# Thirty-two experts fed from HBM: a seventh unit staged ahead, and the staged loads asked for by GpSimd's queue

## What is computed

```python
def moe_ffn(h, w_router, b_router, w_gate_up, b_gate_up, w_down, b_down):
    xt = h.reshape(T, D)                                  # 256 x 1024
    logits = (xt @ w_router) + b_router                   # 32 experts
    top_v, top_i = lax.top_k(logits, TOP_K)               # 4 of them per token
    gates = jax.nn.softmax(top_v, axis=-1)
    ...
    def expert_block(args):
        xb, e = args
        hdn = xb @ w_gate_up[e] + b_gate_up[e]            # 1024 x 2048 weights
        return clamped_swiglu(hdn) @ w_down[e] + b_down[e]  # 1024 x 1024 weights
    ...
    out = jnp.zeros((T, D), y.dtype).at[tok_sorted].add(y[dest] * g_sorted[:, None])

def clamped_swiglu(hdn):
    x_glu = jnp.minimum(hdn[..., :D_EXPERT], SWIGLU_LIMIT)
    x_lin = jnp.clip(hdn[..., D_EXPERT:], -SWIGLU_LIMIT, SWIGLU_LIMIT)
    return x_glu * jax.nn.sigmoid(SWIGLU_ALPHA * x_glu) * (x_lin + 1)
```

## Time and profile before

| what | value |
|---|---|
| median of 3 runs | 2068.12 us (2065.26 to 2071.54) |
| the profiled execution | span 2064.6 us from the first to the last instruction; the page gives no other time of it |
| median less span | 3.5 us |
| PE busy | 1945.9 us, 94% |
| POOL busy | 589.1 us, 29% |
| HBM read | 607.17 MB |
| expert stage | from about 226 us to about 1204 us of the span |

### The profile page before, as it was taken

One profiled execution on the slowest core, in us unless ns is written; L12 is line 12 of the kernel. 1 busy time (PEld: TensorE's weight loads), 2 busy tenths in 40 slices (PEclk: granted clock), 3 DMA queues, 4 the chain that ended last, 5 costly groups with the idle time before them and its releaser, 6 DMA issues.

```text
span 2064.6 us, 28177 instructions
## 1 busy us (share of the span) xinstructions
PE 1945.9 (94%) x10657; PEld 1193.4 (58%) x10658; DVE 892.1 (43%) x1387; ACT 721.6 (35%) x1182; POOL 589.1 (29%) x622
## 2 busy tenths in 40 slices
PE   5998899989999999999999889999999999999998
PEld 2975333323333333333332269788888898898887
DVE  4645312111222221111211156557797575576983
ACT  2544111101111111111111055664665466646662
POOL 3230243443342433424433504000233021000440
PEclk7998899999999999999999989999999999999999
DMA  9999599999898999999999965345456554544653
GB/s 341 299 360 367 227 420 417 417 418 418 342 419 326 419 418 417 367 395 417 419 417 417 418 230 200 123 152 196 152 190 208 169 185 132 174 170 137 197 194 120
DMA packets 203044, 609.34 MB, mean 295 GB/s; under 512 B 10458, under 2 KB 115054, under 8 KB 166384
## 3 DMA queue, kind: packets, MB, share of 16 engines
q1 hardware_dynamic: 197360, 585.14, 74.2%
q0 software_dynamic: 5280, 22.19, 3.1%
q10 hardware_dynamic: 328, 0.95, 0.1%
HBM read 607.17 MB, written 9.26 MB: 299 GB/s over the span
## 4 chain that ended last, share of the span: by engine, by line
PE 69%; DMA 11%; SPq 7%; DVE 6%; ACT 4%; issue 2%; POOL 1%; ACTq 0%; DVEq 0%
PE bank L903 21%; PE bank L1256 14%; PE bank L940 10%; DMA side<-in_w_gate_up 9%; PE bank L1280 8%; PE bank L942 5%; SPq L740 5%; PE bank L1207 2%; SPq L747 2%; PE bank L1220 1%; DMA ring<-in_w_down 1%; DVE split L1739 1%; PE bank L1010 1%; PE bank L1248 1%; ACT split L2167 1%
## 5 line engine op out<-in xcount | busy, mean ns | idle before, releaser
L1256 PE MATMUL bank<-ring,qkv 128*64 128x512 f32 x2240 | 502.9, 597 | 34.0 <-POOL ring L2423 33.9
L1256 PEld LDWEIGHTS bank<-ring,qkv 128*64 128x64 f32 x2240 | 151.8, 137 | 367.0 <-issue 265.1
L1739 DVE TENSOR_TENSOR split<-ring,split 128x2048 fp32r<-128x2048 f32 x104 | 249.1, 2395 | 115.4 <-ACT split L2167 115.3
L940 PE MATMUL bank<-hT_both,split 128*128 128x512 f32 x800 | 283.2, 399 | 7.1 <-DVE split L1739 7.1
L1280 PE MATMUL bank<-ring,qkv 128*64 128x512 f32 x1120 | 248.5, 595 | 1.2 <-DMA ring<-in_w_down 1.0
L2167 ACT ACTIVATE split<-ring 128x2048 fp32r<-128x2048 f32 x104 | 199.1, 1915 | 130.9 <-PE bank L903 126.2
L942 PE MATMUL bank<-hT_both,split 128*128 128x256 f32 x800 | 223.6, 280 | 0.0
L1713 DVE TENSOR_SCALAR qkv<-bank 128x512 f32<-128x512 f32 x35 | 24.2, 692 | 443.5 <-PE bank L1256 443.5
L2139 ACT ACTIVATE qkv<-qkv 128x512 f32<-128x512 f32 x35 | 22.1, 631 | 533.5 <-DVE qkv L1713 533.5
L1727 DVE SCALAR_TENSOR_TENSOR out_halves<-bank,small,out_halves 64x512 fp32r<-64x512 f32 x70 | 52.5, 750 | 332.3 <-ACT out_halves L2150 331.8
L940 PEld LDWEIGHTS bank<-hT_both,split 128*128 128x128 f32 x800 | 151.6, 189 | 44.6 <-DVE split L1739 8.4
(11 more groups left out here) (363 smaller groups left out, 3045.5 us busy)
## 6 DMA issues: line engine op xcount, KB each, us to landing
ring<-in_w_down SPq DMA_DIRECT2D x150, 1024.0 KB, 17.2
ring<-in_w_gate_up SPq DMA_DIRECT2D x70, 1024.0 KB, 20.4
probs<-in_w_gate_up SPq DMA_DIRECT2D x62, 1024.0 KB, 18.0
ring<-in_w_in SPq DMA_DIRECT2D x58, 1024.0 KB, 5.5
ring<-in_w_up SPq DMA_DIRECT2D x44, 1024.0 KB, 5.1
qkv<-in_w_gate_up SPq DMA_DIRECT2D x31, 1024.0 KB, 21.7
consts<-in_w_gate_up SPq DMA_DIRECT2D x31, 1024.0 KB, 20.5
side<-in_w_gate_up SPq DMA_DIRECT2D x31, 1024.0 KB, 22.4
```

The source lines that it names most:

```text
L940: pe.matmul(b[:, :].rearrange("p (h t) -> p h t", h=2), w_high[:, k, rows], hT_both[:, :, k, :], start=(k == 0), stop=False, skip_group_ch ...
L1256: last = pe.matmul(hidden[q][CAP * j:CAP * j + CAP, :], xgT[:, k % 4, k // 4, :], unit_at(k)[:, c:c + 512], start=False, stop=(k == KC - 1 ...
L1739: dve.tensor_tensor(low, unit_at(u % RING_L), high.bitcast(F32), ALU.subtract).then_inc(low_done, 1)
```

## The change

`STAGED` becomes 7: unit 6 gets a second buffer too. Its memory comes from scratch rows that now share: `glu` lies on `xrow`, `act_row` and `brows` on `sig`, and `bdown` on the new staged buffer. Since `glu` and `xrow` are one row, ACT's `rows_out` waits until DVE has made the activation (`act_ready`). SP asks for expert 1's unit 6 once the slot tables are filled (`slots_filled`). The staged loads of experts 2 to 31 are no longer issued by SP: POOL issues each right behind its own copy of the same unit of the expert before (`load_staged`, behind a wait for that copy and one more one-column add), and signals them in `landed_staged`; the ones of expert 1 stay with SP and signal in `landed_early`. SP's loop only has `load_direct(e)`, for units 7 to 11. POOL's loop is cut into expert 1, experts 2 to 30 and expert 31.

```diff
-STAGED = 6
+STAGED = 7
...
-        xrow, glu, lin, sig = (moe(512) for _ in range(4))
-        bdown, staged_qkv = moe(D)[0:EXPERTS, :], moe(UNIT)
+        xrow, sig = (moe(512) for _ in range(2))
+        staged_qkv = [moe(UNIT) for _ in range(2)]
+        bdown = staged_qkv[0][0:EXPERTS, 0:D]
         assert at[0] <= 6144
-        brows, act_row = glu, lin
+        glu, brows, act_row = xrow, sig, sig
...
-        staged_at = [probs_t[:, 0:UNIT], probs_t[:, UNIT:2 * UNIT], hT_t[:, :], const("bands"), staged_qkv, side[:, :]]
+        staged_at = [probs_t[:, 0:UNIT], probs_t[:, UNIT:2 * UNIT], hT_t[:, :], const("bands"), staged_qkv[1], side[:, :], staged_qkv[0]]
...
-            def load_staged(e, u):
-                sp.dma_start(staged_at[u], hidden_rows(e)[:, u, :]).then_inc(landed_staged[u], 16)
+            def load_early(u):
+                sp.dma_start(staged_at[u], hidden_rows(1)[:, u, :]).then_inc(landed_early[u], 16)
...
             sp.wait_ge(*full("logits4"))
-            load_staged(1, 2)
+            load_early(2)
             sp.wait_ge(*emptied("list"))
+            sp.wait_ge(slots_filled, 1)
+            load_early(6)
             load_direct(1)
             with sp.Fori(2, EXPERTS) as e:
-                for u in range(STAGED):
-
-                    sp.wait_ge(landed_moe[u], e + 15)
-                    load_staged(e, u)
                 load_direct(e)
...
             def rows_out(n):
                 act.wait_ge(gathered, n)
+                if type(n) is not int or n > 1:
+                    act.wait_ge(act_ready, n - 1)
                 act.activation(xrow, banks[6][:, :], ACT.Copy).then_inc(xrow_ready, 1)
...
-            with pool.Fori(1, EXPERTS) as e:
+
+            def load_staged(e, u):
+
+                pool.wait_ge(landed_moe[u], e + 15)
+                pool.tensor_tensor(passed[:, STAGED + 1 + u:STAGED + 2 + u], zeros[:, 0:1], zeros[:, 0:1], ALU.add)
+                rows = w_gate_up[0, bass.ds(e, 1)].rearrange("e (k p) n -> (e p) k n", p=P)
+                pool.dma_start(staged_at[u], rows[:, u, :]).then_inc(landed_staged[u], 16)
+
+            def fill_units(e, more):
+
+                landed_of, landings = (landed_staged, 16 * e - 16) if type(e) is not int or e > 1 else (landed_early, 16)
+
                 blocks_before = pool.value_load(lists[0:1, bass.ds(BLOCKS + e, 1)], min_val=1, max_val=BLOCKS)
-                landings = pool.snap(16 * e)
+                if type(e) is not int:
+                    landings = pool.snap(landings)
                 pool.wait_ge(moe_used[0], blocks_before)
-                pool.tensor_tensor(passed[:, STAGED:], zeros[:, 0:1], zeros[:, 0:1], ALU.add)
+                pool.tensor_tensor(passed[:, STAGED:STAGED + 1], zeros[:, 0:1], zeros[:, 0:1], ALU.add)
                 pick_rows(bass.ds(4 * e, 4))
                 for u in range(STAGED):
                     pool.wait_ge(landed_moe[u], 16)
-                    pool.wait_ge(landed_staged[u], landings)
+                    pool.wait_ge(landed_of[u], landings)
                     pool.wait_ge(moe_used[u], blocks_before)
                     pool.tensor_tensor(passed[:, u:u + 1], zeros[:, 0:1], zeros[:, 0:1], ALU.add)
                     pool.tensor_copy(unit_at(u), staged_at[u]).then_inc(landed_moe[u], 1)
+                    if more:
+                        load_staged(e + 1, u)
                 pool.wait_ge(landed_moe[STAGED - 1], e + 16)
+
+            fill_units(1, True)
+            with pool.Fori(2, EXPERTS - 1) as e:
+                fill_units(e, True)
+            fill_units(EXPERTS - 1, False)
```

More of the change, by code:

```diff
@@ L448, in build @@
         top, negtop, total, scale = (little(TT * HEADS) for _ in range(4))
-        zeros, spare, passed = little(T), little(1), little(STAGED + 1)
+        zeros, spare, passed = little(T), little(1), little(2 * STAGED + 1)
         def q4(a):
@@ L603, in build @@
         landed_staged = [sem(f"landed_staged{s}") for s in range(STAGED)]
+        landed_early = [sem(f"landed_early{s}") for s in range(STAGED)]
         bands_in, pick_ready = sem("bands_in"), sem("pick_ready")
@@ L758, in _ @@
             for u in (0, 1):
-                load_staged(1, u)
+                load_early(u)
             sp.wait_ge(*full("bout3"))
-            load_staged(1, 4)
+            load_early(4)
             sp.wait_ge(unit_done, 33 + 1)
```

## The result

The changed kernel takes **2112.11 us** (median of 4 runs, 2109.2 to 2115.2) against 2069.49 us for the kernel before on the same chip: ratio 1.021, 95% interval 1.0194 to 1.0227, 43 us slower. The profiled execution took 2115.2 us, with a span of 2113.5. The forecast was 2115.

What follows compares the result with a forecast made beforehand. Transfers bound one-block experts (30.08 us against 26.39), PE two-block ones (52.78). The stage ends 48.8 us later, 2 return: span 2064.6 + 46.8 = 2111.4, median 3.5 above, 2115; own range 2098 to 2130, 8 in 10 from 2062.

Steps and rivals of the forecast that it cites:

- The term that decides: Two load queues: POOL's gets 0.64 of the bandwidth, SP's 0.36, so five direct units take 32.9 us against 26.39.
- The rival of even shares: Both queues get half of the bytes, five direct units take 25 us: no change, 2064 us (2058 to 2071), chance 0.13.
- The sum: Expert stage: 27 experts x 30.08, one 26.39, three x 52.78 from 254.32; end at 1251.2, middle taken 1249.
- Idle at the two-block experts: Experts 9, 13 and 20: some 20 us without transfers at each, against 7.8, 10.2 and 8.0 before.
- The start: First expert: POOL asks for expert 2's units earlier, so about 9 of 21.3 us idle go away.
- The single experts: One-block experts: each starts from one same state and takes 30.08 us, 27 of them 812.2 us.
- 30 us apart: Sign in the expert stage: POOL's starts 30 us apart, and 53 us at three places.
- down units landing 20 us and more after their issue: Sign in SP's queue: down units land 20 us and more after issue, staged ones in under 10.
- The last block: End of the expert stage: the last one-block expert finds all loaded and takes 26.39 us.
- POOL's unit: POOL's copy, add and DMA issue: some 2.9 us per unit, seven 20 us of 26.39; cost taken as 0.
- The return behind the stage: Layer 1's first weights there earlier: returns at most 6.48 us of PE's wait, at least nothing; 2 taken.
- The clock: PE after long waits at the down units: some 3 us lost per restart, three allowed, 10 us from above.

Runs made afterwards that it cites:

- even_rows: The changed kernel with the down units laid out in 8 KB rows too, same queues, requests and bytes: 2066.34 us, ratio 0.9984.
- AHEAD = 6: The kernel before, one queue, with all six staged units of the next expert asked for ahead of this one's down units: 2102.26 us, ratio 1.0172.

## Why the prediction was right, point by point

**The term that decides** was the sharing between the queues, taken from one landing in the kernel before: bands in 3.9 us, POOL's share 0.64. The experiments confirm what followed from it: uneven rows 43 us, equal rows 2 to 12, one queue 0. That they take turns packet by packet, a row each, is read from the equal counts, 607 and 608 packets with 65% of the bytes in POOL's queue; the order of single packets on one engine isn't in these views. The prediction's 0.64 from a single landing was a thin basis, and it held. The rival of even shares had its time right (2064; even_rows gave 2066), only this kernel isn't in it. The Trainium skill ("DMA: Bandwidth & Descriptors", "SWDGE vs HWDGE vs iDMA") puts a packet at 4096 bytes at most by preference; were it always so, the shares would have been even whatever the row, but in this trace a row of 8 KB is one packet. Its sentence that issuing from several engines only saves the sequencer's time ("Issuing engines are not separate DMA queues") leaves out what happened here: the second queue changed the order of service, and that cost 2%.

**The sum** gave 1249 for the end of the down products; it is 1246.05. Idle at the two-block experts was put at 20 us each; it is 19.8, 17.4 and 16.2. The start gave 11.1 us back where I had 9. The single experts don't go as the prediction has it, each from the same state and 30 us apart. POOL's starts from expert 10 to expert 14:

```profile
524.26 0.39 POOL L2407 CAST pick_low<-consts 128x256 fp32r x1
550.66 0.39 POOL L2407 CAST pick_low<-consts 128x256 fp32r x1
577.06 0.39 POOL L2407 CAST pick_low<-consts 128x256 fp32r x1
612.51 0.39 POOL L2407 CAST pick_low<-consts 128x256 fp32r x1
665.31 0.39 POOL L2407 CAST pick_low<-consts 128x256 fp32r x1
```

Two intervals are 26.4 us, PE's own time, the third is 35.4, then comes 52.8 for the next two-block expert. So the waits fall on some experts in large pieces. All 31 starts lie between 228.7 and 1196.6; less three of 52.8 that leaves 29.98 us as the mean of 27, against 30.08 in the sum. So the sum holds, and the sign "30 us apart" holds only in the mean. The sign "down units landing 20 us and more after their issue" didn't separate the kernels: the median is 18.5 us, and it was 17.2 before; the staged ones, 8.8 to 12.4 now, were at 18 to 22.

**That 2115 came so near to 2112.11** is partly luck. The stage is 45.9 us longer, not 48.8; behind it nothing came back where I took 2; the profiled execution was 3 us slower behind L880's start (856.1 us against 853.1), which nothing forecast; and its time, 2115.2, is the highest of the four.

**The last block** that finds all loaded is there: PE waits for nothing after 1190.

**POOL's unit** was put at 2.9 us and takes 3.27. POOL in order of time, one unit to the next:

```profile
613.00 1.88 POOL L2437 COPY ring<-probs 128x2048 f32<-128x2048 f32 x1
614.96 0.19 POOL L2418 TENSOR_TENSOR small<-small 128x1 f32<-128x1 f32 x1
615.55 0.57 POOL L2420 DMA_DIRECT2D probs<-in_w_gate_up  x1 [0.40 <-issue]
616.14 0.20 POOL L2436 TENSOR_TENSOR small<-small 128x1 f32<-128x1 f32 x1
616.27 1.89 POOL L2437 COPY ring<-probs 128x2048 f32<-128x2048 f32 x1
```

The part missed is 0.4 us for the address registers. Seven units take 22.9 us, under 26.39, so the 0 stood.

**The return behind the stage**, 2 us, did not come: from the last down product's end to L880 it is 11.30 us now and 11.31 before. It was a guess within bounds, and 0 was right.

**The clock** was allowed up to 10 us. PE in order of time at the last long wait, then PEclk over the three stretches around it:

```profile
1182.57 1.94 PE L1280 MATMUL bank<-ring,qkv 128*64 128x512 f32 x8 [1.52 <-DMA ring<-in_w_down]
1189.81 3.54 PE L1280 MATMUL bank<-ring,qkv 128*64 128x512 f32 x8 [5.30 <-DMA ring<-in_w_down]
```

```profile
1181.00:1189.00 8.00, 1.99 (x10) 0.48 (x8) 0.00 (x0) 0.00 (x0) 3.06 (x5) 1.00 1.02 421
1189.00:1194.00 5.00, 4.19 (x11) 1.40 (x12) 0.00 (x0) 0.50 (x1) 0.00 (x0) 0.66 1.01 418
1194.00:1198.00 4.00, 4.00 (x21) 1.35 (x21) 2.12 (x4) 0.87 (x2) 1.55 (x4) 1.00 1.01 408
```

After 5.30 us idle, eight products take 3.54 us in place of 1.94, with the granted clock partly at its lower level of 1.2 GHz. In all L1280 is busy 23 us more than before (271.7 against 248.5) and L1256 14 us less (488.6 against 502.9), so the net is 9 us. Over the whole stage the granted clock is 0.97; in the kernel with `AHEAD = 6`, which waits as long in all (65.8 us) but in 86 pieces of at most 2.9 us, it is 1.00, and that kernel loses 34 us, not 43. The stage in the changed kernel and in that one:

```profile
250.00:1246.00 996.00, 925.33 (x4100) 324.09 (x4096) 182.40 (x306) 129.65 (x206) 597.91 (x892) 0.97 0.94 383
```

```profile
250.00:1238.00 988.00, 918.31 (x4114) 318.41 (x4110) 205.90 (x309) 133.50 (x211) 378.44 (x422) 1.00 0.95 389
```

So up to some 9 of the 43 us may belong to the clock; the two kernels differ in more than that, and no run isolates it.

## What to carry to other kernels

A prefetch is worth only what it leads at the moment when it is wanted. Here the loads of two queues were served a row from each in turn, so in the proportion of their row lengths and not in the order of need. So before a stream is moved to a second queue, compare what share the urgent loads will keep with the time they have; if it isn't enough, keep one queue, ordered by need, or make the rows equal. And an engine that asks sooner isn't a gain while the transfers are the bound: look for stretches where they stand still.

## What was unexpected of the hardware

Row length changes the bandwidth of 1 MB loads even at 4 KB and more: the full slices show 422 GB/s when all experts' rows are 8 KB, 417 to 420 with both lengths, and 410 when all are 4 KB. Over a stage of 384 MB this was worth 6 us one way and 17.6 the other. And a DMA of POOL with an address from a register costs it 0.57 us and some 0.4 ahead of it, whereas one with a constant address costs 0.56 alone.
